# Unread bfloat16 products ahead of TensorE's waits, and high and low products grouped in the wide feed-forward helper

## What is computed

```
h = rms_norm(x, g0)
m = parallel_conv_mla(h, ...)            # block 1: w_in, short convolution, 8-head attention, w_out
x = x + rms_norm(m, g1)
x = x + rms_norm(square(relu(rms_norm(x, g2) @ mlp_w1[0])) @ mlp_w2[0], g3)     # d_ff 4096
...
m = conformer_conv(h, ...)               # block 2: w_pw1, 31-tap convolution, layer_norm, silu, w_pw2
x = x + rms_norm(square(relu(h @ mlp_w1[1])) @ mlp_w2[1], g)
...
m = hybrid_mixer(h, ...)                 # block 3: w_in_2, 4 heads of differential attention,
                                         # 8 heads with compressed, selected and window branches, w_out_2
x = x + rms_norm((silu(h @ w_gate) * (h @ w_up)) @ w_down, g)                   # d_ff 2816
```

## Time and profile before

| | us |
|---|---|
| median of 3 runs | 994.23 (993.13 to 994.96) |
| the profiled execution | 994.82 |
| its span, first to last instruction | 993.0 |
| mean granted clock of TensorE | 0.975 of full |
| weight bytes read | 159.31 MB |

### The profile page before, as it was taken

One profiled execution on the slowest core, in us unless ns is written; L12 is line 12 of the kernel. 1 busy time (PEld: TensorE's weight loads), 2 busy tenths in 40 slices (PEclk: granted clock), 3 DMA queues, 4 the chain that ended last, 5 costly groups with the idle time before them and its releaser, 6 DMA issues.

```text
span 993.0 us, 12881 instructions
## 1 busy us (share of the span) xinstructions
PE 940.1 (95%) x4885; PEld 783.2 (79%) x4885; DVE 699.3 (70%) x699; ACT 241.6 (24%) x501; POOL 309.3 (31%) x187
## 2 busy tenths in 40 slices
PE   4998899999999999899999999899999989999996
PEld 4877578888888678688888888788776778888885
DVE  5778738877777755749877677678768378677674
ACT  2113423110101500323010101355556221111112
POOL 5343024344445242123344443400000233333331
PEclk9999799999999999899999999999969999999999
DMA  8661413654566264415555555366304127565641
GB/s 299 233 221 64 152 61 129 240 183 169 179 245 228 96 209 146 127 43 175 206 176 210 204 213 173 127 210 214 107 1 128 42 90 250 173 205 172 197 141 43
DMA packets 82438, 160.89 MB, mean 162 GB/s; under 512 B 4942, under 2 KB 40633, under 8 KB 82400
## 3 DMA queue, kind: packets, MB, share of 16 engines
q1 hardware_dynamic: 82112, 159.78, 47.3%
q10 hardware_dynamic: 288, 0.59, 0.2%
HBM read 159.31 MB, written 1.05 MB: 161 GB/s over the span
## 4 chain that ended last, share of the span: by engine, by line
PE 76%; DVE 14%; ACT 4%; POOL 2%; issue 2%; DMA 1%; DVEq 0%; SPq 0%; POOLq 0%; ACTq 0%
PE ps L1680 74%; DVE w_lo L700 3%; PE ps L1684 2%; ACT arena L1318 1%; DVE x_res L766 1%; DVE nrm L776 1%; POOL st L607 1%; DVE w_lo L714 1%; POOL st L606 1%; DMA x_res<-in_x 1%; ACT arena L1590 1%; DVE st L1128 0%; DVE arena L819 0%; DVE act_hl L785 0%; DVE nrm L745 0%
## 5 line engine op out<-in xcount | busy, mean ns | idle before, releaser
L700 DVE TENSOR_TENSOR w_lo<-raw,w_hi 128x2048 fp32r<-128x2048 f32 (+3 forms) x134 | 317.6, 2396 | 43.0 <-POOL w_hi L681 23.3
L1680 PE MATMUL ps<-act_hl,w_hi 128*128 128x512 f32 (+1 forms) x1088 | 329.9, 375 | 11.6 <-DVE act_hl L785 7.3
L1680 PE MATMUL ps<-act_hl,w_lo 128*128 128x256 f32 (+1 forms) x1024 | 256.8, 280 | 0.0
L1680 PEld LDWEIGHTS ps<-act_hl,w_hi 128*128 128x128 f32 x1088 | 189.9, 192 | 52.6 <-DVE act_hl L785 8.7
L1680 PE MATMUL ps<-w_hi,act_hl 128*128 128x512 f32 (+2 forms) x656 | 186.6, 385 | 5.9 <-DVE w_lo L700 4.8
L588 POOL TENSOR_SCALAR w_hi<-raw 128x2048 fp32r<-128x2048 f32 x56 | 136.2, 2433 | 172.5 <-PE ps L1680 172.5
L1680 PE MATMUL ps<-w_hi,hl 128*128 128x512 f32 (+2 forms) x680 | 186.6, 384 | 0.0
L1680 PEld LDWEIGHTS ps<-act_hl,w_lo 128*128 128x128 f32 x1024 | 179.9, 189 | 0.9
L1680 PEld LDWEIGHTS ps<-w_hi,hl 128*128 128x128 f32 (+1 forms) x680 | 125.7, 189 | 24.6
L1680 PEld LDWEIGHTS ps<-w_hi,act_hl 128*128 128x128 f32 x656 | 118.7, 189 | 32.5 <-issue 5.4
L573 POOL TENSOR_SCALAR w_hi<-raw 128x2048 fp32r<-128x2048 f32 (+5 forms) x39 | 78.0, 2004 | 177.2 <-PE ps L1680 156.0
(11 more groups left out here) (180 smaller groups left out, 724.7 us busy)
## 6 DMA issues: line engine op xcount, KB each, us to landing
raw<-in_mlp_w SPq DMA_DIRECT2D x64, 1024.0 KB, 5.2
raw<-in_w_gate SPq DMA_DIRECT2D x22, 512.0 KB, 3.9
raw<-in_w_up SPq DMA_DIRECT2D x22, 512.0 KB, 4.9
raw<-in_w_down SPq DMA_DIRECT2D x11, 1024.0 KB, 5.0
raw<-in_odd_w_pw SPq DMA_DIRECT2D x16, 512.0 KB, 5.1
raw<-in_w_in SPq DMA_DIRECT2D x8, 1024.0 KB, 5.4
raw<-in_even_w_in SPq DMA_DIRECT2D x6, 1024.0 KB, 8.5
raw<-in_even_w_out SPq DMA_DIRECT2D x4, 1024.0 KB, 5.1
```

Source lines behind the costliest of these rows:

```text
L700: tt(w_lo[slot_of(n)][:, 0:w], raw[slot_of(n)][:, 0:w], w_hi[slot_of(n)][:, 0:w].bitcast(F32), ALU.subtract).then_inc(S("w_split"), 1)
L1680: return pe.matmul(o, l, r, start=start, stop=stop, skip_group_check=True)
```

## The change

A new helper `keep_warm(bank, n)` issues n products of `mask_id` with `mask_neg` repeated four times (bfloat16, 512 columns) into a PSUM bank that nobody reads. It is called at five places: in `turn_normed` (10 before the wait for tile 0, 4 before that for tile 1); in block 1's attention after the scores of heads 1 and 2 (5 and 4, with a wait for `mask` at head 0); in `w_in_2` ahead of the fourth piece (9); and in block 3's attention after `scores_of(4)` (8), after `compressed_scores()` and after `turn_of(5)` (4 each). In `wide`, two output banks are taken together: all eight high products, then all eight low ones. The high ones of the first two banks wait for `w_hi` only, and `w_split` is waited for ahead of the first low one.

```diff
+                def keep_warm(bank, n):
+
+                    for _ in range(n):
+                        mm(ps[:, bank, :], mask_id[:, :], mask_neg[:, :].unsqueeze(1).to_broadcast([P, 4, P]), True, True)
+
...
-                    arrived(n, turn_, per)
                     wh = w_hi[slot_of(n)][:, 0:k * cols].rearrange("p (k n) -> p k n", k=k)
                     wl = w_lo[slot_of(n)][:, 0:k * cols].rearrange("p (k n) -> p k n", k=k)
                     width = moving.shape[2]
-                    for c in range(cols // P):
-                        if read and c % 2 == 0:
-                            pe.wait_ge(S(read[0]), read[1 + c // 2])
-                        for kk in range(k):
-                            act_k = moving[:, lhs_k0 + kk, :]
-                            s = slice(c * P, (c + 1) * P)
-                            mm(ps[:, bank + c, 0:width], wh[:, kk, s], act_k, first and kk == 0, False)
-                            ins = mm(ps[:, bank + c, 0:width // 2], wl[:, kk, s], act_k[:, 0:width // 2],
-                                     False, last and kk == k - 1)
-                        if out and c == 1:
+                    for c0 in range(0, cols // P, 2):
+                        if read:
+                            pe.wait_ge(S(read[0]), read[1 + c0 // 2])
+                        for part in range(2):
+                            if c0 == 0:
+                                pe.wait_ge(S("w_hi" if part == 0 else "w_split"), turn_ * per + n + 1)
+                            for c in (c0, c0 + 1):
+                                s = slice(c * P, (c + 1) * P)
+                                for kk in range(k):
+                                    act_k = moving[:, lhs_k0 + kk, :]
+                                    if part == 0:
+                                        mm(ps[:, bank + c, 0:width], wh[:, kk, s], act_k, first and kk == 0, False)
+                                    else:
+                                        ins = mm(ps[:, bank + c, 0:width // 2], wl[:, kk, s], act_k[:, 0:width // 2],
+                                                 False, last and kk == k - 1)
+                        if out and c0 == 0:
                             ins.then_inc(S("front_out"), 1)
...
                         for m in range(M):
+                            if k == 0:
+                                keep_warm(SPEC + 1, 10 if m == 0 else 4)
                             pe.wait_ge(S("normed"), normed[0] + m + 1)
...
                         ins.then_inc(S("scores"), 1)
+                        if t == 0:
+                            pe.wait_ge(S("mask"), 1)
+                        elif t < 3:
+                            keep_warm(UP, 6 - t)
...
                         need_lows(lows[0] + 2 * m + j // 2 + 1)
+                        if m == 0 and j == 3:
+                            keep_warm(UP + 3, 9)
                         tall(n + j, ACC, act_hl, 2 * j, j == 0, j == 3, 2, 792, tiles=(m,), free=m == 1)
...
                 scores_of(DH)
+                keep_warm(ACC, 8)
                 turn_of(3)
...
                 compressed_scores()
+                keep_warm(UP + 2, 4)
                 turn_of(DH)
...
                         turn_of(t - 1)
+                        keep_warm(UP + 2, 4)
                         turn_compressed()
```

## The result

The changed kernel takes 985.16 us (median of 4 runs, 983.54 to 985.69) where the kernel before took 994.6 beside it. The ratio is 0.9895, with a 95% interval of 0.9865 to 0.9925. The profiled execution took 985.58 us, its span is 983.8. The forecast was 983.7, the range 978.0 to 990.0.

What follows compares the result with a forecast made beforehand. TensorE was taken to bound the MLPs and last feed-forward, with half-clock stretches elsewhere. Gains of 4.4 + 1.2 + 1.35 + 3.6 + 0 + 0 = 10.55 us off the 994.23 median gave 983.7 us, range 978.0 to 990.0.

Steps and rivals of the forecast that it cites:

- grouping: In wide, 800 high and low pairs on the chain at 348 ns in place of 353: 4.4 us gained.
- later wait for `w_lo`: Second piece of the last feed-forward's second block: high products fill the 1.57 us wait; 1.2 us gained, w_lo of down late next.
- start of `w_in_2`: Nine products fit in the 2.28 us wait and keep the clock at full: 1.35 us gained.
- block 3: Attention: full clock to the compressed scores, 4.7 us earlier, then the clock falls again near turn_of(5): 3.6 us gained.
- block 1's attention: The clock still falls, near 104.5 in place of 101: 0 gained, with 2.2 us as the other bound.
- `turn_normed`: Products free; 0.65 us gained, or a loss of 1.05 if the clock falls ahead of pw2; taken as 0.
- Rival 3: The order of high and low products in wide is free, by the skill's rule: 988.1 us, chance 0.10.
- the other branch: Block 3: the clock does not fall again near turn_of(5), giving 5.4 us in place of 3.6.
- Rivals 2 and 4: 2: products don't hold the clock, 990.7 us, chance 0.13; 4: they run at half clock, in the way, 1001.0, 0.04.
- Rival 1: The clock holds at all five places, behind the products too: 979.0 us, chance 0.23.

Runs made afterwards that it cites:

- group_only: The changed kernel without its 48 unread products, so only the grouping of wide and its later wait for w_lo: 992.05 us against 993.47, ratio 0.9968.
- products_only: The 48 unread products of the changed kernel, with wide in its old order as before the change: 990.26 us, ratio 0.9954.
- group_early_wait: The changed kernel without unread products and with the wait for w_split back ahead of the loop in wide: 992.16 us in one run.
- fill_norm_only: The changed kernel with five more unread products after each norm ahead of the MLPs and the last feed-forward: 985.57 us, ratio 0.9911.
- nine_before_turn: The changed kernel with nine unread products ahead of turn_of(5) in place of the four behind it: 981.72 us, ratio 0.9867.
- run 218: Not a run or kernel: the words come from "the products run 218 ns apart", the spacing of the unread products at full clock.
- all_waits_filled: The changed kernel with products ahead of further waits: block 1's attention, after norms, pw2, and nine ahead of turn_of(5) replacing four behind: 981.14 us, ratio 0.986.
- changed_again: The changed kernel's same text, run once more without any edit: 986.1 us over six runs, ratio 0.99.

## Why the prediction was right

The time, 985.16, lies 1.5 us above the forecast. By its own steps, against the ledger (forecast, measured in the profiled execution):

| step | forecast | measured |
|---|---|---|
| grouping | 4.4 | 4.3 |
| later wait for `w_lo` | 1.2 | 1.0 |
| start of `w_in_2` | 1.35 | 1.33 |
| block 3 | 3.6 | 3.94 |
| block 1's attention | 0 | -0.1 |
| `turn_normed` | 0 | 0.60 |
| after the last norm | not named | -1.5 |
| first 97 us | 0 | -0.4 |
| sum | 10.55 | 9.2 |

**Grouping.** 1.28 and 1.31 us in the MLPs, 0.27 in the second block of the last feed-forward and 1.42 in the rest: 4.3, of which the MLPs' 448 pairs give 5.8 ns each; the 64 pairs of `w_in` can't be told from the spread of the first 97 us. `group_only` has the same without any added product, `products_only` next to nothing. Rival 3, the order being free, falls. It came from the Trainium skill ("TensorE: Matmul & The Clock Gate", section "Back-to-back issue gap"). The section gives columns over the clock and 2.5 ns as the gap of a product by itself; the prediction's "whatever stands beside it" goes beyond that, since the section also says that in a stream of weight loads and products both set the spacing. These traces don't agree with the 325 ns that the rule gives for this pair of shapes, with 353 ns a pair in turn and 348 grouped.

**Later wait.** 1.0, told apart by `group_early_wait`. The next late thing was the one named, `w_lo` of `down`, with 0.60 us idle. The term was 0.2 too large.

**Start of `w_in_2`.** Right in size, and in mechanism: without the products nothing is gained, with them 1.32 to 1.34 in every kernel that has them in this size.

**Block 3.** The forecast had the clock fall again near `turn_of(5)`, behind a wait it put at 2.5 us and which was 2.12, and `products_only` shows the other branch at 5.5 against 5.4 forecast. Both branches exist; the changed kernel's two traces took the first. Of the 0.3 more than forecast, 0.1 is the four products (1.70 in place of 1.82) and the rest that the clock was back at 729.65, during the turn ahead of `out_of(4)`, so that this took 0.46 us in place of 0.63.

**Block 1.** The stretch began at 105.01, near the 104.5 forecast, with the wait named. The half clock before was also longer than the 6.7 us that the prediction opens with, 10.2 from 101.0. The outcome of nothing was right for this trace and no property of the kernel: in other executions of the same code the gain is 1.3 or 2.4. That 0 came out here is luck. The step should have stood as three outcomes with a chance for each.

**`turn_normed`.** 0.60, near the upper bound of 0.65, since the wait ahead of `pw2` lost no clock though it was the longest of all:

```profile
416.75 0.74 PE L1680 MATMUL ps<-w_hi,act_hl 128*128 128x512 f32 x2 [2.44 <-DVE act_hl L732]
```

Little of it is shown to be the products': `group_only` and `group_early_wait`, without any, gained 0.55 and 0.54 there with a half-clock stretch of 3.4 us, where the one trace of before has 6.8. So most of the 0.60 may be what that execution of before happened to lose. What failed is the step that set a loss of 1.05 against this, from one wait of 2.28 us that had lost the clock elsewhere: a wait's length alone doesn't decide.

**What was missed** is the stretch at 794.5, 1.5 us, in two of two traces of the changed kernel. TensorE waits 1.20 us there for `act_hl`, before and after the change alike; before, it lost nothing. The first row is of before, the second of after:

```profile
802.27 4.10 PE L1680 MATMUL ps<-act_hl,w_hi 128*128 128x256 f32 x32 [1.20 <-DVE act_hl L785]
794.28 5.59 PE L1680 MATMUL ps<-act_hl,w_hi 128*128 128x256 f32 x32 [1.20 <-DVE act_hl L785]
```

The prediction costed the clock only at the five places that the change touches. It named the reason it could be wrong, that the place may differ from run to run, but gave it no price. `fill_norm_only` prices it: the stretch there can be removed and another appears, with no gain in the median. One thing about it repeats: the stretch there, beginning at 794 to 799 us, stood in all five traces in which the clock fell between 724 and 728 us and that wait was left as it was, and in none of the five others that left it so (`nine_before_turn`, `products_only`, before, and the two without products). Why a fall 70 us earlier should go with it, no run here shows.

The small miss in time, 1.5 us, is thus a sum of larger ones with both signs: 0.3 and 0.6 more than forecast in block 3 and `turn_normed`, 1.5 and 0.4 less after the last norm and in the first 97 us, where the changed kernel adds no product.

Rivals 2 and 4 fall too: `products_only` is faster than before, with 5.5 us in block 3, and the products run 218 ns apart in the waits. Rival 1, at 979.0, was not this kernel, but `all_waits_filled` comes to 981.14 with extra products.

## What to carry over

Fill a wait of TensorE ahead of the instruction that waits, and not behind it, with no more products than the wait is long: the same idea gave 3.9 us with four products behind `turn_of(5)` and 6.35 with nine ahead of it (one trace of the second). Cost a clock effect as a chance and not as a yes or no, and sum over the whole program: a single trace of each kernel can differ by 1.5 to 3 us at places that nobody touched, so a table of where the difference grows, over several traces, is worth more than the median. Order products by shape in dense loops: 5.7 ns a pair is little, but it repeats exactly, 1.28 us in the first MLP in each kernel that has it.

## What the runs showed of the hardware

- **Where the clock falls differs between executions.** Half-clock stretches began at 65, 155 to 158, 339 to 343, 721 to 727 and 794 to 799 us in some executions and not in others of the same code there. After waits of 1.21 and 1.51 us it fell in one trace and not in another; after the 2.44 us ahead of `pw2` it fell in no trace of a kernel with the products; in `all_waits_filled` it fell at 721 us with no wait over 0.33 us in the 12 us before. What decides it, these runs leave open; none of them shifted a stage in time and left its waits and products as they were.
- **A stretch costs what it lies on.** 3.4 us at half clock on dense TensorE work cost 1.5 to 1.6 us (342.9 and 794.5), and 6.8 us cost 3.2. Among waits it cost less: 3.4 us in block 1's attention cost 1.1 (a gain of 1.3 with it in `changed_again`, 2.4 without in `fill_norm_only`).
- **Products of 32 weight columns held the clock** at `w_in_2` and in the first half of block 3 as well as ones of 128, in the one run made.
- **High and low products in turn** are 353 ns a pair, grouped 348: alternating 512 and 256 columns costs 5 to 6 ns a pair beyond the sum of the two. Why, no run here shows.
